# Eight sample rows of every split projection: three terms side by side in column groups instead of one after another

## Chip, cores and metric

One core of one Trainium2 chip. The metric is device time in microseconds (us) of one execution of the whole kernel. The engines are TensorE (PE, with its weight loads PEld), VectorE (DVE), ScalarE (ACT), GpSimd (POOL) and SyncE (SP), which issues most DMAs.

## What is computed

One decoder layer for a prompt of 1024 rows and eight sample rows that share its weights. The parts that matter here:

```python
h = rmsnorm(x, norm1_g[l]) * (1 + sc1) + sh1
q_a, k_a, v_a, g_lr, r_a, q_d, k_d, v_d = split_proj(jnp.matmul(h, w_in[l]))
...                                  # GLA mixer on q_a..r_a, dilated attention on q_d, k_d, v_d
mix = jnp.concatenate([o_a, o_d.astype(x.dtype).reshape(B, S, H_D * DH_D)], axis=-1)
x = x + g1 * jnp.matmul(mix, w_o[l])
h = rmsnorm(x, norm2_g[l]) * (1 + sc2) + sh2
x = x + g2 * moe(h, router_w, router_b, moe_w_gate[l], moe_w_up[l], moe_w_down[l])
```

All values are float32. The kernel reaches that precision with float16 matmuls: each operand is split into a high and a low half, and a product is the sum of three terms, high x high, high x low and low x high.

## The kernel before

**Tiles.** The 1032 rows are nine row tiles: t = 0 to 7 with 128 prompt rows each, and t = 8 (the code's PT) with the eight sample rows. A projection of a row tile takes, for each of eight blocks k of 128 inputs, three matmuls into one PSUM bank: the row tile is the stationary operand and the weights move. `products` (L1600) issues them at L1605, L1606 and L1607. Tile 8 is treated like the others, with a stationary operand of eight columns (the form `128*8` in the profile), so its matmuls move as many weight columns as those of a full tile.

**Stages.** (0) up to about 246 us: modulation vectors, then a loop over the nine row tiles in which `project_gla` (L1610) makes 784 columns in two banks (512 + 272) and in two halves of k; between the halves stands `first_slot`, after them `second_slot`, which run the linear-attention chunks two tiles behind. ACT stores columns 0 to 511 (L811), DVE the other 272 (L1180). Then `project_first` (L1697) makes the 384 columns of the first pair of attention heads for t = 0 to 8. It needs weights that ACT splits (L788, high) and DVE splits (L1158, low). (1) to about 670 us: six head pairs c. (2) to about 885 us: output projection `project` (L1903), residual, second norm, router. (3) the experts. All engines meet in a barrier between stages.

**The loop over a head pair.** Each engine has its own `attend(c)` with eight slots i (query blocks), and its order is the program's order. PE (L1845) does in slot i: the first entry of `FILL[i]`, `turn(2i)` (transposes of the probabilities of head 0, L1807), `scores(i+1)` (L1793), `turn(2i+1)` of head 1, the remaining entries of `FILL[i]`, then `values(i)` (L1821) and the turn of the denominators (L1827). `FILL` lists halves (t, h) of the projections of the next pair, `project_half(c+1, t, h)` (L1763), that are put between the steps of the attention. In slot 7 there is no entry; PE turns q and k of the next pair there (`turn_qk`, L1779).

ACT (L903) does in slot i: copies of the transposed probabilities (`keep_pT`, L867), the two exponentials for slot i+1 (`exp_tile`, L859), `high_out` (L878), then the stores (`store_qkv`, L793) of the row tiles whose second half stands in `FILL[i]`, then `keep_rden` (L873), and in slot 6 a split of the weights of the pair after next (L788).

DVE (L1328) does in slot i: `bias_max` of head 1 (L1264, L1267), the scaling of the last output (L1283), its part of `keep_pT` (L1274, from slot 4 on), the reciprocals (L1278), `bias_max` of head 0 for slot i+1. In slot 7, after the reciprocals: `split_low(c+2, 0)` (L1158), `store_qT(c+1)` (L1251), its copy of head 1 (L1274), on which `values(7)` waits.

**Banks.** `proj_bank` gives row tiles 7 and 8 the same PSUM bank, 7. The first half of tile 8 therefore waits until ACT has stored tile 7:

```python
before = {0: 0, 2: 1, 3: 2, 4: 3, 5: 4, 6: 5, 7: 7, 8: 8}[t]
pe.wait_ge(qkv_ok, c * NT + before)
```

`qkv_ok` counts the stored row tiles, nine (NT) for each pair.

**End of stage 2.** PE's order is `project(8, 0)`, `turn_rows(7)` (waits for the normed tile 7, DVE L1412), `project(8, 1)`, `route(7)`. After the second half DVE multiplies the PSUM result of tile 8 by the gate (L1399), adds the residual (L1400), ACT squares it, DVE norms it (L1411, L1412), PE turns it and the router follows.

Of the kernel before, what the change touches and what calls it, by code (L numbers as in the profile page):

```python
# [33 lines left out]
D = 1024  # L34
# [30 lines left out]
FILL = (((0, 1), (1, 0), (1, 1)), ((2, 0), (2, 1), (3, 0)), ((3, 1), (4, 0), (4, 1)), ((5, 0), (5, 1)),  # L65
        ((6, 0), (6, 1)), ((7, 0), (7, 1)), ((8, 0), (8, 1)), ())

# [59 lines left out]
def build(nc, x_prompt, x_sample, state_gla, cache_win_k, cache_win_v, c_prompt, c_sample, w_ada, b_ada, norm1_g,  # L127
# [26 lines left out]
    with ExitStack() as ctx:  # L154
# [211 lines left out]
        hT_ok = sem("hT_ok"); act_link = sem("act_link"); dve_link = sem("dve_link");   # L366
        wG_in = [sem(f"wG_in{j}") for j in range(2)]; gproj_ps = sem("gproj_ps"); gprojA = sem("gprojA"); gprojB = sem("gprojB")
        gA_ps = sem("gA_ps"); gB_ps = sem("gB_ps"); gl_ok = sem("gl_ok"); lnz_ok = sem("lnz_ok"); loga_ok = sem("loga_ok")
# [354 lines left out]
        def _(act):  # L723
# [66 lines left out]
            def store_qkv(c, t, b):  # L790
                n = rows_of(t)
                act.wait_ge(qkv_ps, c * NT + (t + 1))
                A(qkv[0:n, t], bank(b, 384, n), ACT.Copy, scale=1.0 / WS).then_inc(qkv_ok, 1)  # L793

# [5 lines left out]
            for t in range(NT):  # L800
                n = rows_of(t)
                if t >= 2:
                    after_b(t)
                if t + 2 < NT:
                    rms(t + 2)
                if t + 1 < NT:
                    high_hT(t + 1)
                if t >= 2:
                    after_a(t)
                act.wait_ge(gproj_ps, t + 1)  # L810
                A(proj[0:n, t, 0:512], bank(4, 512, n), ACT.Copy, scale=1.0 / WS).then_inc(gprojA, 1)  # L811
            act.wait_ge(wP_in, 48)
# [140 lines left out]
            for t in range(NT):  # L953
                n = rows_of(t)
                act.wait_ge(res_ok, t + 1)
                lk.done(A(xr[t % 2][0:n], X1[0:n, t], ACT.Square, accum_out=ss[0:n, t:t + 1]))
# [97 lines left out]
        def _(dve):  # L1054
# [55 lines left out]
            sc, lo = Steps(dve, scaled_ok), Steps(dve, loga_ok)  # L1110

            def after_b(i):
                dve.wait_ge(gB_ps, i - 1)
# [51 lines left out]
            for t in range(NT):  # L1165
# [13 lines left out]
                dve.wait_ge(gproj_ps, t + 1)  # L1179
                v.tensor_scalar(proj[0:n, t, 512:GW], bank(5, GW - 512, n), 1.0 / WS, None, ALU.mult).then_inc(gprojB, 1)  # L1180
                if t + 2 < NT:
# [48 lines left out]
            for c in range(2):  # L1230
                dve.wait_ge(gm_hi, c + 1)
                v.tensor_tensor(mixl[:, c, 0:S], banks[:, 1024 * c:1024 * c + D], mixh[:, c, 0:S], ALU.subtract)
            for c in range(2):
                dve.wait_ge(gm_hi, c + 3)
                v.tensor_tensor(mixl[:, c, S:TOK], bank(6 + c, NB), mixh[:, c, S:TOK], ALU.subtract)
# [92 lines left out]
            def attend(c):  # L1328
                more = c + 1 < PAIRS
                for i in range(PT):  # L1330
# [22 lines left out]
                    if i + 1 < PT:  # L1353
                        bias_max(c, 2 * i + 2)
                    elif more:
                        if c + 2 < PAIRS:
                            split_low(c + 2, 0)
                        store_qT(c + 1)
# [32 lines left out]
            for t in range(NT):  # L1391
# [6 lines left out]
                b = 2 * (t % 2)  # L1398
                lk.done(v.tensor_tensor(X1[0:n, t], banks[0:n, 512 * b:512 * b + D], g, ALU.mult))  # L1399
                v.tensor_tensor(X1[0:n, t], X1[0:n, t], xr[t % 2][0:n], ALU.add).then_inc(res_ok, 1)  # L1400
# [172 lines left out]
        def _(pe):  # L1573
# [26 lines left out]
            def products(out, t, wh, wl, ks, first, last):  # L1600

                n = rows_of(t)
                tok = slice(t * P, t * P + n)
                for k in ks:
                    mm(out, hTh[:, k, tok], wh(k), start=(first and k == ks[0]), stop=False)  # L1605
# [4 lines left out]
            def project_gla(t, j):  # L1610
# [8 lines left out]
                for o, w, bb in ((0, 512, b), (512, GW - 512, b + 1)):  # L1619
                    last = products(bank(bb, w, n), t, lambda k: wGh[:, k, o:o + w], lambda k: wGl[:, k, o:o + w],  # L1620
                                    range(4 * j, 4 * j + 4), j == 0, j == 1)
# [75 lines left out]
            def project_first(t):  # L1697
                if t == 0:
                    pe.wait_ge(wlo_ok, 4)
                    pe.wait_ge(gprojA, NT)  # L1700
                elif t == 1:
                    pe.wait_ge(gprojB, NT)
                else:
                    pe.wait_ge(qkv_ok, t - 1)
                products(bank(4 + t % 2, 384, rows_of(t)), t, lambda k: w0h[:, k], lambda k: w0l[:, k], range(KC), True,
                         True).then_inc(qkv_ps, 1)
# [56 lines left out]
            def project_half(c, t, h):  # L1763
# [4 lines left out]
                if t == 0:  # L1768
                    pe.wait_ge(wlo_ok, c * 2 + h + 3)
                last = products(bank(b, 384, rows_of(t)), t, lambda k: wPh[:, k], lambda k: wPl[:, k],  # L1770
                                range(4 * h, 4 * h + 4), h == 0, h == 1)
# [3 lines left out]
            def turn_qk(c):  # L1775
                pe.wait_ge(qkv_ok, c * NT + NT)
                for j in range(2):
# [125 lines left out]
            def project(t, h):  # L1903
                tok = slice(t * P, t * P + rows_of(t))
                if h == 0:
                    if t >= 2:
                        pe.wait_ge(res_ok, t - 1)
                    if t == PT:
                        pe.wait_ge(smix_ok, 2)
                out, cols = bank(2 * (t % 2) + h, 512, rows_of(t)), slice(512 * h, 512 * h + 512)  # L1910
                for k in range(KC):
                    mm(out, mixh[:, k, tok], wOh[:, k, cols], start=(k == 0), stop=False)  # L1912
# [191 lines left out]
```

## Time and profile before

| what | value |
|---|---|
| time, median of 3 runs | 1361.9 us (1361.71 to 1362.45) |
| time of the profiled execution | 1366.18 us |
| its span, first to last instruction | 1364.6 us |
| PE busy | 1126.3 us (83% of the span) |
| DVE busy | 702.5 us (51%) |
| ACT busy | 607.8 us (45%) |
| mean granted TensorE clock | 0.918 of 2.4 GHz |

How to read a profile: times run from the span's start. A row of a timeline has the start, the length, the engine, the line of the kernel, the operation with its shapes, how many neighbouring ones are merged, and in brackets how long the engine sat idle before it and what ended that. A matmul's length goes to its modelled end; back-to-back matmuls overlap, so the time that one takes is the distance between two starts. A float32 matmul appears as two.

### The profile page before, as it was taken

What the parts mean: (1) busy time and instruction counts of PE and PEld (TensorE: products, weight loads), DVE (VectorE), ACT (ScalarE), POOL (GpSimd) and SP (SyncE); (2) the same over time, 40 slices, a digit from 0 to 9 for tenths busy, and PEclk for the clock granted to TensorE, in tenths of its full rate; (3) what the DMA queues carried; (4) which work ended last, traced back from release to release, by engine and by line L of the source; (5) the groups of instructions that cost most, each with busy time, mean ns of one, the idle gap of its engine ahead of it and who ended that gap; (6) DMA issues with size and microseconds to landing.
All of it is one profiled execution on the core that took longest, in us unless ns stands there. A gap on an engine that the chain in (4) does not pass through costs nothing.

```text
span 1364.6 us, 18815 instructions
## 1 busy us (share of the span) xinstructions
PE 1126.3 (83%) x6935; PEld 630.3 (46%) x6936; DVE 702.5 (51%) x1099; ACT 607.8 (45%) x939; POOL 118.8 (9%) x135
## 2 busy tenths in 40 slices
PE   3799999898989898996799980089999999999800
PEld 0255656465656566664445540034444444444400
DVE  2356545454444444346333336257558658655557
ACT  2256553444454545345311121157557557555434
POOL 0000000000000000000100003320112111111032
PEclk9799988899999999998889995589999999999955
DMA  9664410605050413822325310569868798768255
GB/s 356 245 215 149 129 49 10 185 1 155 1 147 10 119 37 96 306 94 64 99 73 170 131 66 7 202 215 381 327 246 307 271 344 322 267 247 332 108 200 188
DMA packets 122341, 234.43 MB, mean 172 GB/s; under 512 B 11079, under 2 KB 54569, under 8 KB 119200
## 3 DMA queue, kind: packets, MB, share of 16 engines
q1 hardware_dynamic: 111760, 200.37, 43.1%
q0 software_dynamic: 7200, 21.06, 4.3%
q10 hardware_dynamic: 3312, 12.06, 2.2%
q8 instruction: 45, 0.74, 0.2%
q14 instruction: 24, 0.20, 0.0%
HBM read 197.60 MB, written 35.64 MB: 171 GB/s over the span
## 4 chain that ended last, share of the span: by engine, by line
PE 65%; DVE 12%; DMA 10%; issue 5%; ACT 5%; POOL 2%; SPq 0%; POOLq 0%; ACTq 0%; DVEq 0%
PE banks L1605 7%; PE banks L1606 7%; PE banks L1607 7%; PE banks L1971 4%; PE banks L1972 4%; PE banks L1973 4%; DMA arena<-in_moe_w_gate_dram 3%; PE banks L1793 3%; PE banks L1821 3%; PE banks L1807 3%; DVE arena L1496 2%; DVE arena L1264 2%; PE banks L1912 2%; DMA arena<-in_w_ada_dram 2%; PE banks L1913 2%
## 5 line engine op out<-in xcount | busy, mean ns | idle before, releaser
L1496 DVE SCALAR_TENSOR_TENSOR arena<-arena 128x2048 f16<-128x2048 f32 x96 | 217.5, 2288 | 82.7 <-ACT arena L972 82.7
L972 ACT ACTIVATE arena<-arena 128x2048 f16<-128x2048 f32 x96 | 180.2, 1906 | 94.2 <-DMA arena<-in_moe_w_up_dram 57.9
L1605 PE MATMUL banks<-arena 128*128 128x384 f16 (+5 forms) x576 | 193.4, 336 | 11.9 <-DVE arena L1158 8.2
L1606 PE MATMUL banks<-arena 128*128 128x384 f16 (+5 forms) x576 | 192.8, 335 | 0.0
L1607 PE MATMUL banks<-arena 128*128 128x384 f16 (+5 forms) x576 | 192.5, 334 | 0.0
L1971 PE MATMUL banks<-arena 128*128 128x512 f16 x368 | 141.5, 385 | 10.5 <-DVE arena L1509 10.4
L1972 PE MATMUL banks<-arena 128*128 128x512 f16 x368 | 141.2, 384 | 0.0
L1973 PE MATMUL banks<-arena 128*128 128x512 f16 x368 | 141.0, 383 | 0.0
L867 ACT ACTIVATE arena<-banks 128x512 f32<-128x512 f32 (+3 forms) x96 | 49.3, 513 | 128.7 <-PE banks L1807 128.7
L1264 DVE CUSTOM_DVE_ANT_0 arena<-banks,arena 128x128 f32<-128x128 f32 (+7 forms) x96 | 72.3, 754 | 45.9 <-PE banks L1793 45.7
L859 ACT ACTIVATE arena<-arena 128x128 f32<-128x128 f32 (+7 forms) x96 | 74.3, 774 | 28.8 <-DVE arena L1267 27.5
L1605 PEld LDWEIGHTS banks<-arena 128*128 128x128 f16 (+1 forms) x576 | 56.8, 99 | 63.6 <-issue 16.7
L1807 PE MATMUL banks<-arena 128*128 128x128 f32 x432 | 66.8, 282 | 19.2 <-ACT arena L867 7.7
L1607 PEld LDWEIGHTS banks<-arena 128*128 128x128 f16 (+1 forms) x576 | 56.8, 99 | 41.1 <-issue 4.1
L1990 PE MATMUL banks<-arena 128*128 128x512 f16 x184 | 70.3, 382 | 5.1 <-DVE arena L1514 5.1
L1606 PEld LDWEIGHTS banks<-arena 128*128 128x128 f16 (+1 forms) x576 | 56.8, 99 | 36.6 <-issue 4.0
L1963 PE MATMUL banks<-arena 128*128 128x128 f32 x192 | 25.8, 279 | 55.7 <-DMA arena<-h_rows,gidx 55.7
L1821 PE MATMUL banks<-arena 128*64 128x128 f32 x864 | 60.8, 288 | 12.6 <-issue 7.0
L1807 PEld LDWEIGHTS banks<-arena 128*128 128x128 f32 x432 | 48.9, 142 | 47.5 <-issue 38.5
L1992 PE MATMUL banks<-arena 128*128 128x512 f16 x184 | 70.5, 383 | 0.0
L1991 PE MATMUL banks<-arena 128*128 128x512 f16 x184 | 70.5, 383 | 0.0
L1793 PE MATMUL banks<-arena 64*128 64x512 f32 (+3 forms) x288 | 61.1, 530 | 2.2 <-DVE arena L1251 2.1
(308 smaller groups left out, 1704.3 us busy)
## 6 DMA issues: line engine op xcount, KB each, us to landing
arena<-in_moe_w_gate_dram SPq DMA_DIRECT2D x32, 1024.0 KB, 8.4
arena<-in_moe_w_up_dram SPq DMA_DIRECT2D x32, 1024.0 KB, 8.3
arena<-in_moe_w_down_dram SPq DMA_DIRECT2D x32, 1024.0 KB, 6.3
arena<-in_w_ada_dram SPq DMA_DIRECT2D x24, 1024.0 KB, 5.3
slot_rows<-arena ACTq DMA_DIRECT2D x23, 512.0 KB, 6.4
out_dram<-arena SPq DMA_DIRECT2D x20, 512.0 KB, 3.1
arena<-in_w_in_dram SPq DMA_DIRECT2D x18, 512.0 KB, 6.6
arena<-in_x_prompt_dram SPq DMA_DIRECT2D x16, 512.0 KB, 8.2
```

The lines of the kernel that those rows point to most:

```text
L972: A(w_hi[s][p // 2][:, (p % 2) * PIECE:(p % 2 + 1) * PIECE], stage[g % RING], ACT.Copy, scale=WS).then_inc(phi_ok, 1)
L1264: v.tensor_tensor_reduce(pB[a % 2][:, 0:n], banks[:, 512 * b:512 * b + n], strip[c % 2][:, hh, P * (PT - 1 - i):D], 1.0, -3e38, ALU.add, A ...
L1496: v.scalar_tensor_tensor(out=w_lo[s][p // 2][:, part], in0=stage[(PIECES * s + p) % RING], scalar=WS, in1=w_hi[s][p // 2][:, part], op0=AL ...
L1605: mm(out, hTh[:, k, tok], wh(k), start=(first and k == ks[0]), stop=False)
L1606: mm(out, hTh[:, k, tok], wl(k), start=False, stop=False)
L1607: done = mm(out, hTl[:, k, tok], wh(k), start=False, stop=(last and k == ks[-1]))
L1793: last = mm(banks[:, at:at + w], qT[r, i * P:(i + 1) * P], kT[r, o:o + w], start=True, stop=True)
L1807: last = tr(banks[:, 2048 + j * P:2048 + (j + 1) * P], pB[a % 2][:, j * P:(j + 1) * P], ident)
L1821: last = mm(banks[r, 3072:3072 + P], vcur[:, j, r], pTB[hh][:, j * P:(j + 1) * P], start=(j == 0), stop=(j == i))
L1971: mm(bank(b), xgTh[:, k], hi, start=(k == 0), stop=False)
L1972: mm(bank(b), xgTh[:, k], lo, start=False, stop=False)
L1973: last = mm(bank(b), xgTl[:, k], hi, start=False, stop=(k == KC - 1))
```

## The change

The three terms of tile 8 go to three column groups of the array: for each k, the three matmuls write to partitions 0 to 7, 32 to 39 and 64 to 71 of the same bank. This applies to `project_gla`, `project_first`, `project_half` and `project`. The three partial results are then summed: ACT copies the first to SBUF as before, and DVE adds the second and the third with one operation each, the second waiting for the first (`add_terms`). Where tile 8 is stored, a new semaphore tells DVE that ACT's copy is there, and `qkv_ok` or `gprojB` is raised by DVE's second addition. In the pair loop DVE's `add_few` stands in slot 7 behind the reciprocals and ahead of `split_low`. `turn_qk` no longer waits for tile 8. `project_first(0)` now waits for `gprojB` of all tiles. In the output projection ACT copies 8 x 1024 to X1, DVE adds twice, and only then multiplies by the gate. Last, `FILL` is changed: the second half of tile 7 moves from slot 5 to slot 6.

```diff
-        ((6, 0), (6, 1)), ((7, 0), (7, 1)), ((8, 0), (8, 1)), ())
+        ((6, 0), (6, 1)), ((7, 0),), ((7, 1), (8, 0), (8, 1)), ())
...
-                A(qkv[0:n, t], bank(b, 384, n), ACT.Copy, scale=1.0 / WS).then_inc(qkv_ok, 1)
+                A(qkv[0:n, t], bank(b, 384, n), ACT.Copy, scale=1.0 / WS).then_inc(qkv_ok if t < PT else few_ok, 1)
...
-                A(proj[0:n, t, 0:512], bank(4, 512, n), ACT.Copy, scale=1.0 / WS).then_inc(gprojA, 1)
+                w = 512 if t < PT else GW
+                A(proj[0:n, t, 0:w], banks[0:n, 2048:2048 + w], ACT.Copy, scale=1.0 / WS).then_inc(gprojA, 1)
...
+                if t == PT:
+                    act.wait_ge(op_ps, NT)
+                    A(X1[0:n, t], banks[0:n, 0:D], ACT.Copy).then_inc(ofew_ok, 1)
                 act.wait_ge(res_ok, t + 1)
...
+            def add_terms(out, ps, scale):
+                lk.done(v.scalar_tensor_tensor(out=out, in0=ps[32:32 + NB], scalar=scale, in1=out, op0=ALU.mult, op1=ALU.add))
+                return v.scalar_tensor_tensor(out=out, in0=ps[64:64 + NB], scalar=scale, in1=out, op0=ALU.mult, op1=ALU.add)
+
+            def add_few(c, b):
+                dve.wait_ge(few_ok, c + 1)
+                add_terms(qkv[0:NB, PT], bank(b, 384), 1.0 / WS).then_inc(qkv_ok, 1)
...
-                v.tensor_scalar(proj[0:n, t, 512:GW], bank(5, GW - 512, n), 1.0 / WS, None, ALU.mult).then_inc(gprojB, 1)
+                if t < PT:
+                    v.tensor_scalar(proj[0:n, t, 512:GW], bank(5, GW - 512, n), 1.0 / WS, None, ALU.mult).then_inc(gprojB, 1)
+                else:
+                    dve.wait_ge(gprojA, NT)
+                    add_terms(proj[0:NB, PT], banks[:, 2048:2048 + GW], 1.0 / WS).then_inc(gprojB, 1)
...
+            add_few(0, 4)
             for c in range(2):
                 dve.wait_ge(gm_hi, c + 3)
...
                     elif more:
+                        add_few(c + 1, proj_bank(PT))
                         if c + 2 < PAIRS:
                             split_low(c + 2, 0)
                         store_qT(c + 1)
...
-                lk.done(v.tensor_tensor(X1[0:n, t], banks[0:n, 512 * b:512 * b + D], g, ALU.mult))
+                if t < PT:
+                    lk.done(v.tensor_tensor(X1[0:n, t], banks[0:n, 512 * b:512 * b + D], g, ALU.mult))
+                else:
+                    dve.wait_ge(ofew_ok, 1)
+                    lk.done(add_terms(X1[0:n, t], banks[:, 0:D], 1.0))
+                    lk.done(v.tensor_tensor(X1[0:n, t], X1[0:n, t], g, ALU.mult))
...
+                if t == PT:
+                    for k in ks:
+                        for g, (x, w) in enumerate(((hTh, wh), (hTh, wl), (hTl, wh))):
+                            done = mm(out[32 * g:32 * g + n], x[:, k, tok], w(k), start=(first and k == ks[0]), stop=(last and k == ks[-1]))
+                    return done
...
-                    pe.wait_ge(gprojA, NT)
+                    pe.wait_ge(gprojB, NT)
...
-                pe.wait_ge(qkv_ok, c * NT + NT)
+                pe.wait_ge(qkv_ok, c * NT + PT)
...
+                if t == PT:
+                    for k in range(KC):
+                        for g, (x, w) in enumerate(((mixh, wOh), (mixh, wOl), (mixl, wOh))):
+                            last = mm(out[32 * g:32 * g + NB], x[:, k, tok], w[:, k, cols], start=(k == 0), stop=(k == KC - 1))
+                for k in range(KC if t < PT else 0):
```

## Rows read from the trace of the kernel before

**Rows 1.** Stretches: length, busy PE, PEld, DVE, ACT, POOL, clock, DMA share, GB/s.

```profile
473.00:535.00 62.00, 61.41 (x469) 39.18 (x470) 28.16 (x80) 28.18 (x66) 0.00 (x0) 1.00 0.21 61
```

**Rows 2.** Timeline of PE, slots 5 to 7 of the third head pair.

```profile
446.62 0.33 PE L1605 MATMUL banks<-arena 128*128 128x384 f16 x1
...
448.66 1.53 PE L1821 MATMUL banks<-arena 128*64 128x128 f32 x24
...
450.63 0.33 PE L1605 MATMUL banks<-arena 128*8 128x384 f16 x1 [0.23 <-ACT arena L793]
...
453.59 1.99 PE L1793 MATMUL banks<-arena 64*128 64x512 f32 x8
455.51 0.98 PE L1807 MATMUL banks<-arena 128*128 128x128 f32 x7
456.43 0.33 PE L1605 MATMUL banks<-arena 128*8 128x384 f16 x1
...
458.47 1.75 PE L1821 MATMUL banks<-arena 128*64 128x128 f32 x28
...
460.37 1.09 PE L1807 MATMUL banks<-arena 128*128 128x128 f32 x8
...
465.84 0.62 PE L1821 MATMUL banks<-arena 128*64 128x128 f32 x7 [1.76 <-issue]
```

**Rows 3.** Timeline of ACT, the same stretch.

```profile
458.88 1.15 ACT L859 ACTIVATE arena<-arena 128x1024 f32<-128x1024 f32 x1 [0.57 <-DVE arena L1267]
...
460.22 0.46 ACT L793 ACTIVATE arena<-banks 8x384 f32<-8x384 f32 x1
```

**Rows 4.** Timeline of DVE, the same stretch.

```profile
447.22 0.43 DVE L1274 COPY arena<-banks 128x256 f32<-128x256 f32 x1
...
461.50 0.69 DVE L1274 COPY arena<-banks 128x512 f32<-128x512 f32 x1 [0.26 <-PE banks L1807]
...
462.25 1.76 DVE L1158 SCALAR_TENSOR_TENSOR arena<-arena 128x1536 f16<-128x1536 f32 x1
...
465.06 0.68 DVE L1274 COPY arena<-banks 128x512 f32<-128x512 f32 x1
```

**Rows 5.** Timeline of PE, first half of tile 8 in stage 0.

```profile
170.67 0.38 PE L1605 MATMUL banks<-arena 128*8 128x512 f16 x1
...
174.75 0.28 PE L1648 MATMUL banks<-arena 128*16 128x128 f32 x1
```

**Rows 6.** Timeline of PE, four column groups (L1588) and one full-width pair (L1665).

```profile
159.67 1.07 PE L1588 MATMUL banks<-arena 128*32 128x512 f32 x8
160.66 0.66 PE L1597 MATMUL banks<-arena 8*128 8x8 f32 x8
...
162.18 1.10 PE L1665 MATMUL banks<-arena 128*128 128x512 f32 x2
163.12 0.59 PE L1666 MATMUL banks<-arena 128*128 128x256 f32 x2
```

**Rows 7.** Groups by line: busy us, mean ns of one, idle before.

```profile
L1524 DVE SCALAR_TENSOR_TENSOR arena<-arena,banks 128x512 f32<-128x512 f32 x23 | 15.7, 684 | 11.1 <-PE banks L1973 11.1
```

**Rows 8.** Timelines of PE and DVE where stage 0 goes over to `project_first`.

```profile
186.80 0.50 PE L1605 MATMUL banks<-arena 128*128 128x384 f16 x1 [3.35 <-DVE arena L1158]
...
181.39 0.43 DVE L1180 TENSOR_SCALAR arena<-banks 8x272 f32<-8x272 f32 x1 [0.96 <-PE banks L1607]
...
183.31 3.43 DVE L1158 SCALAR_TENSOR_TENSOR arena<-arena 128x1536 f16<-128x1536 f32 x2 [1.49 <-ACT arena L788]
```

**Rows 9.** Timeline of DVE at the end of stage 2.

```profile
801.77 1.22 DVE L1412 TENSOR_TENSOR arena<-arena 128x1024 f32<-128x1024 f32 x1
809.50 1.21 DVE L1399 TENSOR_TENSOR arena<-banks,arena 8x1024 f32<-8x1024 f32 x1 [6.51 <-PE banks L1914]
```

**Rows 10.** Stretch table around two idle gaps of PE.

```profile
186.80:192.60 5.80, 5.80 (x19) 2.78 (x20) 2.11 (x8) 0.91 (x3) 0.00 (x0) 0.50 0.30 71
904.30:911.00 6.70, 3.41 (x16) 1.58 (x17) 6.70 (x4) 6.42 (x4) 2.22 (x1) 1.00 0.94 322
```

More of the change, by code:

```diff
@@ L366, in build @@
         hT_ok = sem("hT_ok"); act_link = sem("act_link"); dve_link = sem("dve_link");
-        wG_in = [sem(f"wG_in{j}") for j in range(2)]; gproj_ps = sem("gproj_ps"); gprojA = sem("gprojA"); gprojB = sem("gprojB")
+        wG_in = [sem(f"wG_in{j}") for j in range(2)]; gproj_ps = sem("gproj_ps"); gprojA = sem("gprojA"); gprojB = sem("gprojB"); few_ok = sem("few_ok"); ofew_ok = sem("ofew_ok")
         gA_ps = sem("gA_ps"); gB_ps = sem("gB_ps"); gl_ok = sem("gl_ok"); lnz_ok = sem("lnz_ok"); loga_ok = sem("loga_ok")
@@ L1619, in project_gla @@
                 for o, w, bb in ((0, 512, b), (512, GW - 512, b + 1)):
-                    last = products(bank(bb, w, n), t, lambda k: wGh[:, k, o:o + w], lambda k: wGl[:, k, o:o + w],
+                    last = products(bank(bb, w), t, lambda k: wGh[:, k, o:o + w], lambda k: wGl[:, k, o:o + w],
                                     range(4 * j, 4 * j + 4), j == 0, j == 1)
@@ L1704, in project_first @@
                     pe.wait_ge(qkv_ok, t - 1)
-                products(bank(4 + t % 2, 384, rows_of(t)), t, lambda k: w0h[:, k], lambda k: w0l[:, k], range(KC), True,
+                products(bank(4 + t % 2, 384), t, lambda k: w0h[:, k], lambda k: w0l[:, k], range(KC), True,
                          True).then_inc(qkv_ps, 1)
@@ L1769, in project_half @@
                     pe.wait_ge(wlo_ok, c * 2 + h + 3)
-                last = products(bank(b, 384, rows_of(t)), t, lambda k: wPh[:, k], lambda k: wPl[:, k],
+                last = products(bank(b, 384), t, lambda k: wPh[:, k], lambda k: wPl[:, k],
                                 range(4 * h, 4 * h + 4), h == 0, h == 1)
@@ L1909, in project @@
                         pe.wait_ge(smix_ok, 2)
-                out, cols = bank(2 * (t % 2) + h, 512, rows_of(t)), slice(512 * h, 512 * h + 512)
-                for k in range(KC):
+                out, cols = bank(2 * (t % 2) + h, 512), slice(512 * h, 512 * h + 512)
+                if t == PT:
[3 more added lines that the diff above has]
+                for k in range(KC if t < PT else 0):
                     mm(out, mixh[:, k, tok], wOh[:, k, cols], start=(k == 0), stop=False)
```

## The prediction

> **What bounds the kernel now.** I read the page first for the shares of the engines, then the stretch table, then the timelines of PE, ACT and DVE in the stages where tile 8 is projected. In the pair loop PE is busy 61.41 of 62 us [rows 1]: what is taken off PE there looks like time won. But the timeline of one pair's end shows where PE waits, and for whom [rows 2 to 4]. The reader should see two things. In slot 6, tile 8's first half starts at 450.63 after 0.23 us of waiting for ACT's store of tile 7 (L793), so this store is only just in time [rows 2]. In slot 7, `values(7)` starts at 465.84 after 1.76 us of idle; the profile names no releaser, but DVE's copy L1274 at 465.06 ends at 465.74, 0.1 before, and DVE runs without a break from 461.50 up to there [rows 2, 4]. The pair's end is DVE's chain.
>
> **What a packed projection costs.** Twelve matmuls of 384 columns take 2.04 us (456.43 to 458.47), 0.163 each at full clock; 12 of 512 and 12 of 272 columns take 4.08 [rows 2, 5]. How column groups run is shown by L1588: eight passes of 512 float32 columns in four groups, with the changes of array layout around them, take 0.99 us, while two passes at full width take 0.94 (162.18 to 163.12) [rows 6]. Four run in the time of one, with 0.05 over. So 24 matmuls of 384 columns as eight groups of three take 8 x 0.163 = 1.3, plus 0.2 for group overhead and layout changes: 1.5 instead of 4.0 with the wait. A half of `project_gla` takes 4.08 / 3 + 0.2 = 1.6 instead of 4.08. The bounds are these and no gain at all. For the output projection, 512 of 784 columns of the 4.08 are 2.7 for twelve matmuls, so 24 of 512 columns take 5.3, and packed 2.0.
>
> **What the additions cost.** DVE has no addition of 8 x 384 from PSUM in the trace. A scalar_tensor_tensor with one PSUM operand takes 0.684 for 512 columns [rows 7], a PSUM operation of 8 x 272 takes 0.43 [rows 8] and one of 8 x 1024 takes 1.21 [rows 9], so eight rows cost what 128 do and 384 columns lie between 0.43 and 0.684: I take 0.54, and 1.1 for two that wait for each other. For 784 columns I take 1.0 each, for 1024 columns 1.3 each.
>
> **The pair loop, slot 5.** Up to `turn(11)`, ending at 446.62, nothing moves. Before, the second half of tile 7 filled 446.62 to 448.66. Now `values(5)` comes next and needs DVE's copy, ready at 447.22 + 0.43 = 447.65, so it starts at about 447.74 [rows 2, 4]: 1.1 us idle. `values(5)` takes 1.66 (28 + 4 matmuls take 458.47 to 460.37 = 1.90, this is 24 + 4), the half of tile 7 takes 2.04, `turn(12)` 0.92 (as `turn(13)`, 455.51 to 456.43): `scores(7)` starts at 452.36 instead of 453.59, 1.2 earlier [rows 2].
>
> **Slot 6, the new wait.** The first half of tile 8 now stands behind `turn(13)` and needs ACT's store of tile 7, whose second half has just moved into this slot. ACT's place for stores in slot 6 is behind both exponentials and `high_out`: before, it reached that place at 460.22, right after the exponential at 458.88, which had itself waited for DVE's maximum of `scores(7)` [rows 3]. That is 6.63 after the start of `scores(7)`, and everything in between hangs on it, so it keeps this distance. A 128-row store takes what the 8-row one takes, 0.46; tile 8 can start 6.63 + 0.46 + 0.05 = 7.15 after `scores(7)` started. PE has finished `turn(13)` after 456.43 - 453.59 = 2.84. So PE idles 4.3 us, with `values(6)` and `turn(14)` queued behind the waiting matmul. Then tile 8 takes 1.5 and `values(6)` 1.9: `turn(14)` starts 10.55 after `scores(7)`, where it was 6.78 (460.37 - 453.59). Net of the 1.2: 2.5 us later in each of the five pairs that project a next one.
>
> **Slot 7.** `add_few` stands in DVE's unbroken chain between the reciprocals and `split_low` (462.25) [rows 4]; `values(7)` and the next pair's `scores(0)` wait for its end. It adds its full 1.1 in four pairs; in the fifth there is no `split_low` and DVE has room. Sum of the loop: 4 x 3.6 + 2.5 = 16.9.
>
> **The clock.** After PE's idle gap of 3.35 us the matmuls from 186.80 to 192.60 ran at 0.50, the 1.2 GHz level: 5.8 us, of which half, 2.9, is loss [rows 8, 10]. After the 3.3 us gap at 904.30 (PE busy 3.41 of 6.70) the clock stayed at 1.00 [rows 10]. Each pair gets two long gaps: 4.3 in slot 6, and in slot 7 1.76 + 1.1 = 2.9. Each costs between 0 and 2.9, and I take the middle of these two rows, 1.45: 5 x 2 x 1.45 = 14.5, bounds 0 and 29 (the second gap can't cost that much, as only `values(7)` and `scores(0)` are on the path behind it; 22 is a fair upper end). The Trainium skill, "TensorE: Matmul & The Clock Gate", section "Why this matters for your kernels", says that idle gaps between bursts of matmuls send the clock back to half. By that rule the loop's clock cost would be the upper end, 22, and the time 1399; the trace agrees at 186.80 and not at 904.
>
> **Stage 0.** The two halves of tile 8 save 2 x 2.5 = 5.0 of PE. What follows waits for DVE: L1180 (0.43) becomes two additions of 784 columns behind ACT's copy, 2.0, and stands ahead of `split_low` (3.43 for two), which releases `project_first(0)` at 186.80 [rows 8]. At most 5.0 - 1.6 = 3.4 is won. Since `first_slot(8)` stands between the halves and ACT's exponentials behind it come before its copy, not all of the second half shows: I take -2.3, bounds -3.4 and -1. `project_first(8)` saves 3.9 - 1.5 = 2.4, and `add_few(0)` behind it costs 1.1 ahead of the barrier: -1.3. The barrier's other engines are earlier.
>
> **End of stage 2.** `project(8, 0)` ends 3.3 earlier (5.3 becomes 2.0), but `turn_rows(7)` waits for L1412, ending at 802.99, so this becomes idle [rows 9]. `project(8, 1)` wins 3.3. Then ACT's copy of 8 x 1024 (about 1.0 with its semaphore) and two additions of 1.3 stand ahead of the multiplication that started at 809.50 [rows 9]: 3.7 - 3.3 = +0.4 (3.7: 1.0 and 2.7 with the waits between). The new 3.3 us gap may halve the clock for `project(8, 1)`: +1.45, bounds 0 and 2.9.
>
> **Sum.** Against the profiled execution (1366.18, span 1364.6): -2.3 - 1.3 + 16.9 + 14.5 + 0.4 + 1.45 = +29.6, 1395.8. The median of the runs lies 4.3 below it: 1361.9 + 29.6 = 1391.5, and I say 1391.
>
> **Rivals.**
> (a) *The clock holds.* The same waits, no loss at half clock: -3.6 + 16.9 + 0.4 = +13.7, 1375.6. For it: the 904 row. Against: 186.80 [rows 10].
> (b) *Faster, because PE's work is the pair's length.* If ACT's store of tile 7 were done before `turn(13)` ends, at 455.2 in the shifted time, PE would not wait, and 2.5 us of PE work comes off each pair: 1361.9 - 12.5 - 3.6 = 1345.8 at best. For it: PE busy 61.41 of 62. Against: ACT's place for the store is reached at 460.22, 1.2 less when shifted, and an ordered queue cannot bring it forward. The Trainium skill, "TensorE: Matmul & The Clock Gate", Part 3, gives 2.38x for three column tiles; an estimate by it on the 42 us of 8-row matmuls (144 x 0.163 + 2 x 4.08 + 2 x 5.3) is 24 us off, 1338, if PE alone counted.
> (c) *The groups don't run side by side.* Then tile 8 keeps its 4 us and all the waits come on top: 1391.5 + 5 x 2.4 in the loop + 6 in stage 0 + 3.3 at the end = 1413. Against: L1588 [rows 6].
> (d) *No difference*: gains of stage 0 cancel a wait that is much shorter than I read, 1362.
>
> **How the numbers follow.** Forecast 0.62 (its own range 1377 to 1404: clock cost 0 to 22 and the bounds of the stages), (a) 0.18, (b) 0.10, (c) 0.05, (d) 0.05. About 0.2% (2.7 us) is what a measurement can tell from no change. Slower: 0.62 + 0.18 + 0.05 = 0.85; faster 0.10; same 0.05. The range reaches from (a) less 4 for its bounds, 1371, to 1405 and leaves out (b), (c) and (d).
>
> **What would show it.** PE should sit idle some 4.3 us ahead of tile 8's first half, released by ACT's store (L793 here); 1.1 us ahead of `values(5)`; 2.9 us ahead of `values(7)`, with two additions of 0.54 in DVE's chain; each pair should last 3.6 us longer, and more with the clock; the clock should show more stretches at 0.50 in the loop; each group of three 384-column matmuls should start within some 0.17 us of the next. The forecast is wrong if the store of tile 7 comes before the exponentials, or if tile 8's first half starts right behind `turn(13)`.

## The result and the profile after

The kernel after takes 1396.51 us (median of 4 runs, 1393.71 to 1399.71), the kernel before on the same chip 1361.81: a ratio of 1.0255, 95% interval 1.0226 to 1.0284. The profiled execution of after took 1397.19 us with a span of 1395.6, which is 31.0 above the span of before. The profile's times below run from the start of that span.

The loop's stretch, at the place in the pairs that [rows 1] shows for before (columns as there), and under it three stretches that begin where PE resumes after a gap:

```profile
490.36:552.36 62.00, 56.75 (x424) 34.62 (x424) 23.99 (x67) 25.21 (x61) 0.00 (x0) 0.95 0.18 51
467.50:471.00 3.50, 3.50 (x32) 1.76 (x34) 0.00 (x0) 0.48 (x1) 0.00 (x0) 0.50 0.23 89
480.00:483.40 3.40, 3.37 (x34) 3.40 (x36) 0.00 (x0) 0.00 (x0) 0.00 (x0) 0.54 1.04 257
402.60:406.00 3.40, 3.37 (x46) 2.78 (x46) 0.69 (x5) 0.48 (x2) 1.04 (x1) 1.00 1.03 252
```

PE's busy time in 62 us fell from 61.41 to 56.75, and the mean granted clock from 1.00 to 0.95. After the gap ahead of tile 8 (the stretch from 467.50) PE ran at 0.50, the 1.2 GHz level; after the gap ahead of `values(7)` it ran almost wholly at that level in one pair (480.00, mean 0.54) and not in another (402.60).

Where PE waits, in the timeline of PE in slots 5 to 7 of the third head pair, which answers to [rows 2]:

```profile
455.83 1.53 PE L1849 MATMUL banks<-arena 128*64 128x128 f32 x24 [0.96 <-ACT arena L868]
...
462.24 0.98 PE L1835 MATMUL banks<-arena 128*128 128x128 f32 x7
467.48 2.73 PE L1630 MATMUL banks<-arena 128*8 128x384 f16 x24 [4.25 <-ACT arena L793]
470.13 3.07 PE L1849 MATMUL banks<-arena 128*64 128x128 f32 x28
...
480.04 2.37 PE L1849 MATMUL banks<-arena 128*64 128x128 f32 x19 [2.97 <-issue]
```

In order these are `values(5)`, `turn(13)`, tile 8 in one packed run of 24 matmuls, `values(6)` and `values(7)`. The three gaps of 0.96, 4.25 and 2.97 us stand in all five pairs to within 0.01, except that the last one is 1.30 in the fifth, where before has 1.09. The engines that they wait for, ACT first, then DVE (to be held against [rows 3, 4]):

```profile
465.61 1.15 ACT L860 ACTIVATE arena<-arena 128x1024 f32<-128x1024 f32 x1 [0.57 <-DVE arena L1284]
...
466.95 0.47 ACT L793 ACTIVATE arena<-banks 128x384 f32<-128x384 f32 x1
...
475.28 0.55 DVE L1117 SCALAR_TENSOR_TENSOR arena<-banks,arena 8x384 f32<-8x384 f32 x1
475.87 0.55 DVE L1118 SCALAR_TENSOR_TENSOR arena<-banks,arena 8x384 f32<-8x384 f32 x1
476.35 1.74 DVE L1170 SCALAR_TENSOR_TENSOR arena<-arena 128x1536 f16<-128x1536 f32 x1
...
479.25 0.68 DVE L1291 COPY arena<-banks 128x512 f32<-128x512 f32 x1
```

ACT's store of tile 7 (466.95) stands behind the exponentials and ends at 467.42, 0.06 before tile 8 starts. On DVE the two additions stand ahead of `split_low` (476.35), and the copy for `values(7)` ends at 479.93, 0.11 before it starts.

Stage 0 goes over to `project_first` (PE, then DVE; [rows 8] show before):

```profile
185.01 0.50 PE L1633 MATMUL banks<-arena 128*128 128x384 f16 x1 [3.77 <-DVE arena L1170]
...
179.65 0.97 DVE L1117 SCALAR_TENSOR_TENSOR arena<-banks,arena 8x784 f32<-8x784 f32 x1 [0.35 <-ACT arena L812]
180.65 0.97 DVE L1118 SCALAR_TENSOR_TENSOR arena<-banks,arena 8x784 f32<-8x784 f32 x1
```

And the end of stage 2 (PE, ACT, DVE; [rows 9] show before):

```profile
830.81 1.56 PE L1956 MATMUL banks<-arena 128*128 128x128 f32 x8 [3.40 <-DVE arena L1435]
832.29 3.06 PE L1942 MATMUL banks<-arena 128*8 128x512 f16 x24
...
845.82 1.02 PE L1956 MATMUL banks<-arena 8*128 8x8 f32 x8 [8.57 <-DVE arena L1435]
...
835.41 1.01 ACT L958 ACTIVATE arena<-banks 8x1024 f32<-8x1024 f32 x1 [1.98 <-PE banks L1942]
...
836.56 1.22 DVE L1117 SCALAR_TENSOR_TENSOR arena<-banks,arena 8x1024 f32<-8x1024 f32 x1 [5.81 <-ACT arena L958]
837.81 1.22 DVE L1118 SCALAR_TENSOR_TENSOR arena<-banks,arena 8x1024 f32<-8x1024 f32 x1
```

Where the 31.0 us arise is read from the starts of the same step in both timelines: -3.9 at the end of stage 0, -3.5 at the first `values(0)`; then +6.5, +5.1, +9.3, +5.1 and +5.2 for the five pairs that project a next one (31.1), +2.9 inside the last pair, +1.8 at the end of stage 2. What is left, -1.3, lies in stage 2 and the experts, where the other kernels below scatter by as much.

### The profile page after: what moved, and what is told of

It is laid out like the page before. It is cut to its first block, busy times and chain, and to the rows that moved or that the text cites. A ratio compares the mean times of both kernels' runs of the same rounds, so it can differ in the third digit from the quotient of the medians.

```text
span 1395.6 us, 18832 instructions
## 1 busy us (share of the span) xinstructions
PE 1118.9 (80%) x6935; PEld 629.8 (45%) x6936; DVE 712.8 (51%) x1114; ACT 609.9 (44%) x940; POOL 122.1 (9%) x135
## 4 chain that ended last, share of the span: by engine, by line
PE 65%; DVE 12%; DMA 9%; ACT 5%; issue 5%; POOL 2%; SPq 1%; POOLq 0%; ACTq 0%; DVEq 0%
PE banks L1633 6%; PE banks L1634 6%; PE banks L1635 6%; PE banks L2003 5%; PE banks L2004 5%; PE banks L2005 5%; PE banks L1849 4%; PE banks L1821 3%; DMA arena<-in_moe_w_gate_dram 3%; PE banks L1835 3%; DVE arena L1281 2%; DVE arena L1519 2%; PE banks L1944 2%; PE banks L1946 2%; PE banks L1945 2%
## 5 line engine op out<-in xcount | busy, mean ns | idle before, releaser
L1633 PE MATMUL banks<-arena 128*128 128x384 f16 (+2 forms) x512 | 172.9, 338 | 11.2 <-DVE arena L1170 8.6
L1634 PE MATMUL banks<-arena 128*128 128x384 f16 (+2 forms) x512 | 171.9, 336 | 0.0
L1635 PE MATMUL banks<-arena 128*128 128x384 f16 (+2 forms) x512 | 171.8, 336 | 0.0
L1849 PE MATMUL banks<-arena 128*64 128x128 f32 x864 | 68.3, 312 | 22.5 <-issue 11.9
L1633 PEld LDWEIGHTS banks<-arena 128*128 128x128 f16 x512 | 51.3, 100 | 56.7 <-issue 15.6
L1849 PEld LDWEIGHTS banks<-arena 128*64 128x64 f32 x864 | 56.7, 158 | 37.8 <-issue 23.8
L1635 PEld LDWEIGHTS banks<-arena 128*128 128x128 f16 x512 | 51.3, 100 | 36.5 <-issue 4.6
L1634 PEld LDWEIGHTS banks<-arena 128*128 128x128 f16 x512 | 51.3, 100 | 32.4 <-issue 3.8
```

What stands on the lines that cost most here:

```text
L1634: mm(out, hTh[:, k, tok], wl(k), start=False, stop=False)
L1635: done = mm(out, hTl[:, k, tok], wh(k), start=False, stop=(last and k == ks[-1]))
L1849: last = mm(banks[r, 3072:3072 + P], vcur[:, j, r], pTB[hh][:, j * P:(j + 1) * P], start=(j == 0), stop=(j == i))
```

## Experiments

The theory: the loss is two waits that the order makes (tile 8 behind ACT's store, because `FILL` moved the second half of tile 7; the additions in DVE's chain), each dearer by the clock that falls behind it, while the column groups themselves do what they say. The rivals: the groups or their sums cost the time themselves, or the order alone is to blame and the groups are worth nothing. Each ratio below is to runs of the kernel before in the same series, whose medians lie between 1361.36 and 1364.22 us.

**fill_back: the change with the order of before.**

```diff
-        ((6, 0), (6, 1)), ((7, 0),), ((7, 1), (8, 0), (8, 1)), ())
+        ((6, 0), (6, 1)), ((7, 0), (7, 1)), ((8, 0), (8, 1)), ())
```

> The changed kernel with FILL as it was before: tile 7's second half again in slot 5, tile 8's halves alone in slot 6. Theory 1 (the moved half of tile 7 makes TensorE wait 4.25 us for ScalarE's store in each of five pairs): the 4.25 us gaps ahead of tile 8 fall to 0.2 or 0.3, the loop loses some 30 us of its 31, time 1356 to 1362. Rival (the column groups and the additions cost the time, the place of tile 7 does not matter): the time stays above 1385.

Measured: 1369.92 us (1366.14 to 1375.49), ratio to before 1.0050 (1.0023 to 1.0077). The order is worth 26.6 of the 34.7 us between the medians, but the time missed the expected range by 8. PE in the third pair:

```profile
449.39 0.82 PE L1630 MATMUL banks<-arena 128*8 128x384 f16 x12 [0.22 <-ACT arena L793]
...
464.17 3.36 PE L1849 MATMUL banks<-arena 128*64 128x128 f32 x32 [2.84 <-issue]
```

Tile 8 no longer waits. The gap ahead of `values(7)` stays at 2.84 us, and `values(7)` now takes 3.36 where it took 1.97 at full clock elsewhere: in the four pairs with this gap a stretch at 0.50 follows each time. With the 1.1 us by which this gap is longer than before thus come another 1.4 in `values(7)` alone, and these four pairs are 0.9 to 2.7 us longer than before; the fifth, whose gap is 1.81, is 1.4 shorter.

**fill_alone: the kernel before with only the new order.** The edit is the reverse of the one above, in the kernel before; there are no column groups and no additions.

> The kernel before with the new FILL and nothing else: no column groups, no additions. Theory 1: the same gap of 4.25 us ahead of tile 8 in each pair, and tile 8 still takes 4 us, so each of the five pairs is 4.9 us longer (2.5 + 2.4) plus what the clock loses (1 to 3 us each): 1391 to 1402. Rival (column groups and additions are the cause): 1362, no change.

Measured: 1398.57 us (1397.45 to 1403.2), ratio 1.0268 (1.0206 to 1.0331). The order alone gives the whole loss. PE in the third pair:

```profile
470.67 0.48 PE L1605 MATMUL banks<-arena 128*8 128x384 f16 x1 [4.25 <-ACT arena L793]
...
483.36 0.88 PE L1821 MATMUL banks<-arena 128*64 128x128 f32 x12 [1.70 <-issue]
```

The gap ahead of tile 8 is the same 4.25 us without any group, and the one ahead of `values(7)` is 1.70, as before the change: the additions are the difference to 2.97.

**add_late: the change with `add_few` moved behind DVE's copy for `values(7)`.**

```diff
-                        add_few(c + 1, proj_bank(PT))
                         if c + 2 < PAIRS:
                             split_low(c + 2, 0)
...
                     keep_pT(c, 2 * i + 1)
+                    if more and i == PT - 1:
+                        add_few(c + 1, proj_bank(PT))
```

> The changed kernel with VectorE's two additions for tile 8 moved in slot 7 from ahead of the weight split to behind the last copy of the transposed probabilities, where VectorE is idle. Theory 1 (the additions stand in the chain that ends the pair): the gap ahead of values(7) falls from 2.97 to 1.8 or 1.9 in four pairs, 4.4 us less plus up to 5 us of clock loss that a shorter gap spares: 1387 to 1392. Rival (the chain has slack, another engine ends the pair): 1396, no change.

Measured: 1390.95 us (1389.69 to 1394.15), ratio 1.0207 (1.0146 to 1.0268). The gap ahead of `values(7)` in the third pair is back to 1.71 us:

```profile
476.86 1.97 PE L1850 MATMUL banks<-arena 128*64 128x128 f32 x32 [1.71 <-issue]
```

By the start of the last pair this kernel is 9.1 us ahead of after, more than the 5.6 between the medians; inside the last pair it loses 7.0 again. That was in no expectation, and the last experiments follow it up.

**keep_busy: the change with unused matmuls in the two long gaps.** Behind `turn(13)` and `turn(15)` of each pair 34 and 22 matmuls write to a PSUM range that nothing reads; they compute nothing of the result.

```diff
+                    if more and i >= 6:
+                        for j in range(34 if i == 6 else 22):
+                            mm(banks[:, 3328:3584], hTh[:, j % KC, 0:P], hTh[:, j % KC, 0:256], start=True, stop=True)
```

> The changed kernel with matmuls whose result nobody uses, put into TensorE's two long gaps of each pair: 34 of 256 columns behind turn(13), 22 behind turn(15), 0.11 us each. They add work but fill waiting time only. Theory 2 (of the loop's 31 us about 17 are waiting and 14 are work done at the half clock that follows the gaps): the clock stays at 1.00 in the loop, gaps shrink to some 0.5 us, time 1379 to 1385. Rival (the waits are all of it, the clock costs nothing): 1396 or a little more.

Measured: 1383.72 us (1379.13 to 1386.6), ratio 1.0155 (1.0095 to 1.0216): 12.8 us faster with more work for PE. The third pair:

```profile
457.93 3.88 PE L1890 MATMUL banks<-arena 128*128 128x256 f16 x34
462.35 1.47 PE L1630 MATMUL banks<-arena 128*8 128x384 f16 x24 [0.54 <-ACT arena L793]
463.75 1.75 PE L1849 MATMUL banks<-arena 128*64 128x128 f32 x28
```

Tile 8 and `values(6)` run at full clock here: 24 packed matmuls from 462.35 to 463.75, 1.40 us, where they took 2.65 (467.48 to 470.13) in after. In these five pairs one stretch at half clock is left, at 329 us, where before has one too. Each pair is 3.53 to 3.57 us longer than before, 17.7 in all. But in the fifth pair the gap ahead of `values(7)` was 1.30 us in after, and 22 unused matmuls last longer than that (the fifth pair of after, then of keep_busy):

```profile
633.02 1.04 PE L1835 MATMUL banks<-arena 128*128 128x128 f32 x8
635.36 1.97 PE L1849 MATMUL banks<-arena 128*64 128x128 f32 x32 [1.30 <-ACT arena L868]
```

```profile
617.97 1.04 PE L1835 MATMUL banks<-arena 128*128 128x128 f32 x8
618.84 2.56 PE L1890 MATMUL banks<-arena 128*128 128x256 f16 x22
621.34 1.97 PE L1849 MATMUL banks<-arena 128*64 128x128 f32 x32
```

From `turn(15)` to `values(7)` it is 2.34 us in after and 3.37 in keep_busy, where `values(7)` follows the unused matmuls without a gap: 1.0 us is their own price. So of the 31.1 us that the five pairs lose, about 16.7 are waits (3.5 in each of four pairs, 2.5 in the fifth) and 14.4 are clock.

**tail_busy: the same at the end of stage 2.** The change with 26 unused matmuls ahead of `turn_rows(7)`; their results are not read.

```diff
+                if t == PT - 1:
+                    for j in range(26):
+                        mm(banks[:, 3328:3584], mixh[:, j % KC, 0:P], mixh[:, j % KC, 0:256], start=True, stop=True)
```

> The changed kernel with 26 unused matmuls of 256 columns in the 3.4 us gap ahead of turn_rows(7) at the end of stage 2. Theory (of the 1.8 us that the end of stage 2 is later, about 0.4 are copy and additions beyond what the matmuls win, the rest is half clock behind the gap): the step from turn_rows(7) to turn_rows(8) goes back from 15.0 us to 13.6. Rival (all 1.8 us are the copy and the additions): it stays 15.0. The total time, 1395, can't tell them apart.

Measured in the one profiled execution (1393.03 us): from `turn_rows(7)` to `turn_rows(8)` 844.60 - 831.22 = 13.38 us, where after has 845.82 - 830.81 = 15.01 and before 13.22.

```profile
831.22 1.09 PE L1956 MATMUL banks<-arena 128*128 128x128 f32 x8 [0.45 <-DVE arena L1435]
832.24 1.90 PE L1942 MATMUL banks<-arena 128*8 128x512 f16 x24
...
844.60 1.02 PE L1956 MATMUL banks<-arena 8*128 8x8 f32 x8 [8.57 <-DVE arena L1435]
```

Copy and additions thus cost 0.16 net of what the groups save, and the clock behind the 3.40 us gap 1.63.

**fill_back_add_late: both mends together.** The edits of fill_back and add_late in one kernel.

> Both edits of the loop together: FILL as before, additions behind the last copy of the probabilities. Theory 1 and the slot-7 chain: with FILL alone put back the loop came out even (each pair 0.4 us shorter by its waits, given back by half-clock stretches behind the 2.84 us gap ahead of values(7)). With the additions out of the chain that gap falls to 1.7 to 1.8, each pair is 1.5 us shorter, and the half-clock stretch behind it goes in most pairs: 1350 to 1358. Rival (the extra time of the kernel with FILL put back comes from the other stages, not from the additions): 1366 to 1370.

Measured: 1365.6 us (1362.95 to 1370.28), ratio 1.0025 (0.9997 to 1.0052). The theory failed in two places. In the five pairs it wins 5.1 us on before, not 7.5 and more: a pair without half clock is 1.3 shorter (70.00 for 71.28), but the gap ahead of `values(7)` falls to 1.98 only, and in three of the four pairs that have it the clock still falls right behind it. In the third pair `values(7)` takes 2.80 where it takes 1.97 at full clock:

```profile
458.86 2.80 PE L1850 MATMUL banks<-arena 128*64 128x128 f32 x32 [1.98 <-issue]
```

And the last pair gives most of it back: at its start this kernel is 8.0 us ahead of before (2.9 of it from stage 0), and after four slots of it 2.7.

**tile8_last and tile8_half_tail: tile 8 as late as it can go, then half of its tail at full width.** The first puts the second half of tile 8 at the end of slot 7, into the gap ahead of `values(7)`. The second also leaves the first 512 columns of tile 8's output projection as before, since PE waits there anyway, so that ACT copies and DVE adds 512 columns instead of 1024. The main lines of both edits, against fill_back_add_late:

```diff
-        ((6, 0), (6, 1)), ((7, 0), (7, 1)), ((8, 0), (8, 1)), ())
+        ((6, 0), (6, 1)), ((7, 0), (7, 1)), ((8, 0),), (None, (8, 1)))
...
-                    A(X1[0:n, t], banks[0:n, 0:D], ACT.Copy).then_inc(ofew_ok, 1)
+                    A(X1[0:n, t, 512:D], banks[0:n, 512:D], ACT.Copy).then_inc(ofew_ok, 1)
...
-                    lk.done(add_terms(X1[0:n, t], banks[:, 0:D], 1.0))
+                    lk.done(add_terms(X1[0:n, t, 512:D], banks[:, 512:D], 1.0))
```

> As the run before, and tile 8's second half goes into the idle time of slot 7, behind turn(15), so its store leaves ScalarE's queue in slot 6. If ScalarE's store of tile 8 in slot 6 (0.46) stands in the chain to values(7), each pair is 0.4 to 0.5 us shorter than in the run before: 2 us in all, 1348 to 1356. Rival (that store has slack): same as the run before.

> As the run before, and in the output projection only the second half of tile 8 (columns 512 to 1023) is in column groups; the first half is one after another, in the time that TensorE would wait for the norm of tile 7 anyway. The copy and the additions are 512 wide instead of 1024. Theory: the end of stage 2, 1.8 us later than before in the changed kernel, comes to 1.5 us earlier than before (no 3.4 us gap ahead of turn_rows(7), so no half clock there, and 2 us less of copying and adding): 3 us less than the run before, 1345 to 1353. Rival (the additions were hidden at the end of stage 2): same as the run before.

Measured: 1363.01 us (1359.56 to 1366.99), ratio 0.9992 (0.9972 to 1.0012), and 1359.75 (1354.9 to 1362.63), ratio 0.9968 (0.9943 to 0.9993). Both missed their ranges. The loop does what was expected of it, a pair without half clock lasts 69.62 us where that of fill_back_add_late lasts 70.00; the loss is in the last pair: they enter the last pair 11.7 and 11.5 us ahead of before and leave its fourth slot 6.0 and 6.1 ahead. The half tail does what was expected of it: from `turn_rows(7)` to `turn_rows(8)` it is 1.8 us shorter than before, where tile8_last is 1.8 longer.

**sp_early: SyncE no longer waits for the late sums.** The last pair of the kernel before, then of fill_back_add_late, each with SP's loads of the output weights and the PE row that waits; of the second also the ACT row between:

```profile
604.35 3.17 SPq L518 DMA_DIRECT2D arena<-in_w_o_dram  x3
621.99 0.52 PE L1807 MATMUL banks<-arena 128*128 128x128 f32 x3 [1.96 <-ACT arena L867]
```

```profile
601.86 3.17 SPq L518 DMA_DIRECT2D arena<-in_w_o_dram  x3
610.98 1.06 ACT L883 ACTIVATE arena<-arena 128x1024 f16<-128x1024 f32 x1 [4.30 <-DMA arena<-in_w_o_dram]
612.62 0.66 PE L1836 MATMUL banks<-arena 128*128 128x128 f32 x2 [5.31 <-ACT arena L868]
```

The pair's first `values(0)` starts 8.0 us earlier than before (605.44 for 613.48), but the loads only 2.5 earlier. ACT waits 4.30 us for a weight that it has to split, its copies for PE are queued behind that, and PE waits 5.31. SP's order is: wait until `qkv_ok` counts all nine tiles, store k and v, load three output weights. With `qkv_ok` raised by DVE's second addition at the end of slot 7, this queue starts later against PE. The edit lets each transfer wait only for what it needs:

```diff
-                sp.wait_ge(qkv_ok, c * NT + NT)
+                sp.wait_ge(qkv_ok, c * NT + PT)
...
                 if c == PAIRS - 1:
+                    sp.wait_ge(few_ok, PAIRS)
                     for k in range(3, 6):
                         load_wo(k)
```

> The kernel fill_back_add_late with SyncE's waits split: the stores of a pair's k and v halves wait for the prompt tiles' copies alone, and the loads of the last three output weights (which land over the split projection weights) wait for the end of the last pair's tile-8 sums, instead of both waiting for the counter that the late sums now raise. Theory: the last pair gives back its gain because these transfers leave SyncE later against TensorE than before; then the 5.31 us gap of TensorE ahead of a scores matmul in the last pair falls to about 2, the last pair loses at most 2 us instead of 5.4, and the time is about 1360 us (1356 to 1363). Rival: the weights are late for another reason (the transfers themselves, or the tile-8 sums that both orders wait for): the gap stays near 5 and the time near 1365.6.

Measured: 1357.93 us (1355.43 to 1361.53), ratio 0.9965 (0.9951 to 0.9979).

```profile
598.15 1.31 SPq L518 DMA_DIRECT2D arena<-in_w_o_dram  x3
608.63 1.04 ACT L884 ACTIVATE arena<-arena 128x1024 f16<-128x1024 f32 x1
615.99 0.87 PE L1837 MATMUL banks<-arena 128*128 128x128 f32 x3 [1.96 <-ACT arena L869]
```

The loads leave 9.3 us ahead of the first `values(0)` (607.49), as they did before the change (613.48 - 604.35 = 9.1); ACT doesn't wait, the 5.31 us gap is gone, and the last pair loses 0.15 where it lost 5.4.

**best: the four mends together.** tile8_half_tail with SP's waits of sp_early, and in the fifth pair tile 8's halves both in slot 6, so that the weights that they read come free earlier.

```diff
+FILL4 = FILL[:6] + (((8, 0), (8, 1)), ())
+
+def fill(c, i):
+    return (FILL4 if c == PAIRS - 2 else FILL)[i]
```

> The kernel tile8_half_tail with the same split of SyncE's waits, and with the last pair's tile-8 sums a slot earlier (both halves of tile 8 as the filling of slot 6 of pair 4, none in slot 7), so that the loads of the last three output weights can leave SyncE earlier. Theory: the 4 us gap in the last pair shrinks and about 5 us come back: 1354 us (1348 to 1357), ahead of both kernels. Rival: the gap doesn't come from SyncE's wait: 1359.75 as before this edit, or more where the packed matmuls in one slot make the sums wait for VectorE.

Measured: 1352.51 us (1350.78 to 1358.6), ratio to before 0.9929 (0.9907 to 0.9952). It beats both kernels. The third pair, PE:

```profile
449.39 1.75 PE L1858 MATMUL banks<-arena 128*64 128x128 f32 x28 [1.12 <-ACT arena L875]
...
457.25 1.97 PE L1858 MATMUL banks<-arena 128*64 128x128 f32 x32 [1.22 <-issue]
```

No gap of PE in the five pairs is over 1.23 us. Half clock is not gone with the long gaps: two stretches are left, from 394.31 and 465.99, each just behind the gaps of 1.04 and 0.74 us that the first slots of the second to fifth pairs have (columns as in [rows 1]):

```profile
466.00:469.40 3.40, 3.40 (x13) 1.62 (x11) 0.36 (x2) 1.39 (x6) 0.00 (x0) 0.50 0.98 281
```

The last pair keeps the lead of 10.7 us with which it starts.

**sp_alone and order_no_groups: is it the groups at all?** The first is the kernel before with SP's split wait only (the weights' loads wait for tile 8's copy). The second is the kernel before with the whole order of best, slots and SP, and tile 8 projected one term after another.

> The kernel before with SyncE's wait split alone: the k and v stores wait for the prompt tiles' copies, the loads of the last three output weights for tile 8's copy as before. If the gap of 1.96 us that TensorE has in the last pair of the kernel before also came from late weights, it goes and the time is about 1360 us; if the transfers there were early enough, no difference: 1362.

> The kernel best without the column groups: the kernel before with the order of best (tile 8's halves in slots 6 and 7, the last pair's earlier) and SyncE's split wait, while tile 8 is projected at full cost as before, without the additions on VectorE. Theory: the groups are worth what they save on TensorE: per pair 2 x 2.04 - 1.5 = 2.5 us, of which about 1.2 are hidden in the gap ahead of values(7); so 5 x 1.3 = 6.5 in the loop, 3.5 in stage 0 and 1.8 at the end of stage 2 are lost against best: 1364 us (1361 to 1367). Rival: the gain of best is the order and the transfers, not the groups: 1353 to 1357.

Measured: 1361.81 us (1354.51 to 1372.88), ratio 0.9997 (0.9967 to 1.0026), and 1361.28 (1356.85 to 1366.07), ratio 0.9995 (0.9971 to 1.0019). Neither differs from before beyond its interval; order_no_groups lies at the lower edge of its expected range. The gap of 1.96 us in the last pair of before stays in sp_alone (1.97), so the transfers were early enough there. A pair without a stretch at half clock lasts, from one `values(0)` to the next (two rows each; before, order_no_groups, best):

```profile
479.28 0.44 PE L1821 MATMUL banks<-arena 128*64 128x128 f32 x4
...
550.56 0.44 PE L1821 MATMUL banks<-arena 128*64 128x128 f32 x4
```

```profile
403.52 0.44 PE L1828 MATMUL banks<-arena 128*64 128x128 f32 x4
...
474.45 0.44 PE L1828 MATMUL banks<-arena 128*64 128x128 f32 x4
```

```profile
472.37 0.44 PE L1858 MATMUL banks<-arena 128*64 128x128 f32 x4
...
542.00 0.44 PE L1858 MATMUL banks<-arena 128*64 128x128 f32 x4
```

That is 71.28, 70.93 and 69.63 us. The order is worth 0.35 a pair and the groups 1.30, the 1.3 that was expected. PE saves 2 x 2.04 - 1.40 = 2.7 us a pair; the rest of it becomes a gap, since `values(7)` follows tile 8 without one in order_no_groups and after 1.22 us in best.

Between the medians of order_no_groups and best lie 8.8 us. In their profiled executions best wins 7.3 in the five pairs (1.3 in each of four, 2.1 in the fifth) and 1.8 at the end of stage 2. That would leave nothing for stage 0, where after, with as much time at half clock as before, was 3.87 ahead of it. What stage 0 is worth here isn't settled: the profiled execution of order_no_groups had 3.4 us at half clock between 180 us and the end of stage 0, those of before and best 13.7, and this hides a difference of that size.

## Why the prediction was right

The prediction said slower, 1391 us, and the time was 1396.51, inside the range and 5.5 above. Between the two profiled executions it said +29.6 and measured +31.0.

- *The pair loop, waits.* Predicted 16.9, measured about 16.7 (keep_busy, without the 1.0 that its unused matmuls cost in the fifth pair). The three gaps were put at 1.1, 4.3 and 2.9 us and are 0.96, 4.25 and 2.97. The fifth pair was given 2.5, since DVE has room for the additions there, and lost about 2.5.
- *The clock.* Predicted 14.5 for ten long gaps, in the middle of two rows of opposite sign; measured about 14.4. That the sum agrees so well is luck, since the picture behind it was not right. There are nine long gaps (the fifth pair has one), and the cost is not the same behind each. All five gaps of 4.25 us were followed by a stretch at 0.50, and of the gaps of 2.97 two, at 323 and 480, while behind those at 403 and 560 the clock held, the two outcomes of [rows 10]. Two more stretches, at 332.94 and 489.95, lie behind the gaps of 1.04 and 0.74 us in the first slot of the next pair, which the prediction doesn't count. In fill_back all four gaps of 2.84 were followed by a stretch at half clock. The Trainium skill, "TensorE: Matmul & The Clock Gate", section "Why this matters for your kernels", warns that idle gaps between bursts of matmuls send the clock back to half; the rows agree in eleven of these thirteen gaps. The kernel keep_busy, which closes the long gaps with unused matmuls, was 12.8 us faster than after.
- *The packed projections.* Predicted 1.5 us for 24 matmuls of 384 columns and 2.0 for 24 of 512; measured 1.40 (462.35 to 463.75) and 1.83 (832.24 to 834.07 in tail_busy). The rival that the groups don't run side by side is refuted: 4.08 to 1.40 is 2.9 times. The Trainium skill, "TensorE: Matmul & The Clock Gate", section "Measured speedup vs the span model", has 2.38 for three column tiles. The measured number here is better, and it decides.
- *The additions.* Predicted 0.54, 1.0 and 1.3 us for 384, 784 and 1024 columns, and 1.0 for ACT's copy; measured 0.55, 0.97, 1.22 and 1.01.
- *Stage 0.* Predicted -2.3 up to `project_first(0)` and -1.3 behind it; measured -1.79 (186.80 to 185.01) and -2.08. The sum, -3.6, came out as -3.87, of which 0.36 is lost again before the first `values(0)`.
- *End of stage 2.* Predicted +0.4 and +1.45 for the clock; measured +0.16 and +1.63 (tail_busy).
- *What was missed.* The change moves the raise of `qkv_ok` from ACT's store to DVE's second addition, and the prediction follows what PE and DVE wait for. SP waits for the same counter ahead of its stores and of the last output weights; the prediction doesn't name it and puts the last pair at nothing. In after this is part of the +2.9 in the last pair (ACT waits 0.95 us for a weight there); in fill_back_add_late, tile8_last and tile8_half_tail the last pair took back 5 to 6 us, until sp_early moved the loads.
- *The step to the median.* I took 4.3 off because the profiled execution of before lies that far above its median. That of after lies 0.7 above its own. The offset belongs to one execution and isn't carried over; without it the prediction would have been 1395.8.
- *Rival (b)*, faster because PE's work is the pair's length, fell as predicted on ACT's place for the store. But it named the right prize: with the waits mended the same groups win, though 9 us and not 16, because part of the saved PE time only turns into a gap (1.22 us in best).

## What to carry over

Before a saving on the busiest engine is booked, follow the step that moves with it: here one half projection moved by a slot cost more than three times what the groups were worth. When the instruction that raises a semaphore changes, list every queue that waits on it, DMA queues included. A new idle gap of TensorE has two prices, the wait and the clock behind it, and unused matmuls in the gap tell the two apart, as long as they end before the gap does: in the fifth pair of keep_busy they didn't, and 1.0 us of their own looked like waiting.

## What the hardware showed

- A gap's clock price isn't a function of its length alone. Gaps of 4.25 us were followed by half clock fifteen times of fifteen (after, fill_alone, add_late), of 2.97 us in two pairs of four in after, of 2.84 in four of four in fill_back, of 1.98 in three of four in fill_back_add_late, and of 1.70 to 1.76 right behind none of the twelve of before, fill_alone and add_late.
- Half clock doesn't need a long gap either. In best, with no gap over 1.23 us in the five pairs, PE fell to 0.50 at 394.31 and 465.99, behind gaps of 1.04 and 0.74; behind the same two gaps at 535.01 and 536.05 the clock held. What decides between them stays open.
- The same three loads of output weights occupied SP's queue for 3.17 us where they went out directly behind the k and v stores (before, fill_back_add_late) and for 1.30 to 1.31 where they went out 8 to 10 us behind these (sp_early with the second store at 589.78, sp_alone, order_no_groups, best). Why wasn't tried.
- Executions of one kernel on one chip spread by up to 1.3% (1355.16 to 1372.91 for 21 of before). The time at half clock is not placed the same in each of them: order_no_groups, whose stage 0 is that of before, ended it 3.0 us earlier (243.03 for 246.02). A single pair of traces may thus differ by 3 us in stage 0 alone.
